# Compression products with the token blocks stationary in four column groups, their weights in a tile of their own, and one product that adds the four parts

## The chip, the cores and the metric

The kernel runs on one NeuronCore of a Trainium2 chip. The metric is the device time of one execution in microseconds (us), taken as the median over several executions. The engines are TensorE (PE, with its weight loads listed apart as PEld), VectorE (DVE), ScalarE (ACT), GpSimd (POOL) and SyncE (SP), which issues most of the transfers.

## The reference

The kernel computes one decoder layer for 256 tokens of width 2048: a mixer of 8 NSA heads and 8 MoBA heads, then cross-attention, then a PEER retrieval over 16384 experts, each followed by a LayerNorm. The change touches one part of the first sub-layer, the compression of the NSA keys and values:

```python
def _compress(raw, pe, w1, w2):
    B, S, G, dk = raw.shape
    c = raw.reshape(B, S // NSA_CMP_STRIDE, NSA_CMP_STRIDE, G, dk)
    blocks = jnp.concatenate([c[:, :-1], c[:, 1:]], axis=2) + pe[:, None, :]
    hid = jax.nn.gelu(jnp.einsum('bnlgd,lde->bnge', blocks, w1))
    return jnp.einsum('bnge,ef->bgnf', hid, w2)
```

It runs once for keys and once for values. Here S is 256, the stride 16, a block 32 tokens (l), the head width 128 (d and e), and there are 2 groups g with 15 blocks n each. So `hid` is a sum over 32 positions l of products with a contraction of 128: (15 x 2 blocks, padded to 32) times (128 x 128 weights of that l). Everything is float32.

## The kernel before

All weights of the first sub-layers come as a stream of slots of 1 MB (128 partitions x 2048 float32). SP loads slot s into place s % 4 of a ring, `ring_raw`. ACT rounds it to `ring_hi` (function `high`, L995), DVE subtracts to get the rest, `ring_lo` (function `low`, L1326), and PE multiplies both parts with the split activations. SP may load slot s when DVE has done slot s - 4 (`lo_ready`, wait at L429 to L432), and ACT may write `ring_hi` of slot s when PE has finished slot s - 4 (`slots_done`).

A column slot (`block_slot`) is one block of 128 output columns: 16 pairs of products, L569 (128x512) and L571 (128x256). ACT copies half of its result out of PSUM (`block_cross`, L1013 and L1015), DVE adds the other half (`block_sum`, L1332), and its semaphore `tb_out` lets PE begin the slot two further on, which uses the same bank. A row slot (`row_slot`, L586) has 24 products of 128x512. The order of the stream at the place of the change is:

- slots 0 to 7: column slots for kc, vc, ks and kw. The first four give `cmpT`, from which DVE builds `blocks` (`blocks_sum`, L1364), 32 tokens positions x 32 columns
- slots 8, 9: the compression weights of the keys (`S_W1K`)
- slots 10 to 17: eight column slots of the NSA queries (`S_NQ`)
- slots 18, 19: the compression weights of the values (`S_W1V`)
- slot 20: the column slot of the gates (`S_GATE`)
- slots 21 to 32: row slots of the values (`S_V`), then the MoBA slots and the rest

The four slots of compression weights are `PLAIN`: ACT and DVE touch only one of their 2048 columns, so that the counts go on, and PE reads them from `ring_raw` as they are. Because PE itself still reads them, SP must wait until PE has done such a slot before it loads the slot four further on:

```python
                if s - R in PLAIN:
                    sp.wait_ge(slots_done, s - R + 1)
```

The 32 products of a compression (L611) have the weights as the stationary operand (128 columns) and `blocks[:, l, :]` (32 columns) as the streaming one, and accumulate in bank 6 or 7. They are interleaved with a column slot: two of them ahead of each of the 16 pairs of slot 10 (keys) and of slot 20 (values). ACT then applies gelu (`hidden`, L1037), and PE multiplies with w2 (L622 for the keys, L650 for the values, over `hid_m`). All orders on the engines are written out by hand; there is no scheduler.

## Time and profile before

| | us |
|---|---|
| median of 3 executions | 1907.45 |
| lowest, highest | 1903.71, 1908.88 |
| span of the profiled execution | 1905.7 |
| PE busy in it | 1866.7 (98%) |
| DVE, ACT, POOL busy | 1459.0, 841.7, 343.3 |

The page of the profile gives no time of its own for the profiled execution beside its span of 1905.7 us; it is 1.75 us below the median. Times in the rows are microseconds from the start of the span. In a row of instructions in order of time, the first number is the start and the second the duration; the ends of matmuls are modelled, and they overlap, so the pace of PE is read from start to start. A product of two plain float32 operands stands in the trace as two weight loads and two matmuls; an operand rounded to fp32r gives one of each.

### The profile page before, as it was taken

The page shows a single profiled execution, that of the slowest core. Times are in us where ns is not written, and L with a number is a line of the kernel's source. Part 1 is how long each engine was busy: PE and PEld are TensorE (multiplying, and loading weights), DVE is VectorE, ACT ScalarE, POOL GpSimd, SP SyncE. Part 2 cuts the span into 40 slices and gives each one's busy share as a digit, 9 for nine tenths or more (in the row PEclk, how much of TensorE's full clock was granted, in tenths as well). Part 3 has the DMA queues.
Part 4 walks back from the last instruction along what each step waited for, and adds up shares of the span by engine and source line. Part 5 has one row for each costly group of instructions (what it writes and reads, how often), then busy time and mean ns, then how long its engine had stood idle before and what let it go on. Part 6 is the DMA issues. An engine that isn't in the chain of part 4 may idle for free.

```text
span 1905.7 us, 25814 instructions
## 1 busy us (share of the span) xinstructions
PE 1866.7 (98%) x10388; PEld 1638.1 (86%) x10388; DVE 1459.0 (77%) x1920; ACT 841.7 (44%) x1138; POOL 343.3 (18%) x216
## 2 busy tenths in 40 slices
PE   7999999999989999999999999999999999999997
PEld 6888888888778999999777889889899898898895
DVE  5444555567674599896888888988988989989886
ACT  4333455444443101223455455455455454454552
POOL 1000122000000001101333223322222323223200
PEclk9999999999989999999999999999999999999999
DMA  8445433755343766889999989999989999989881
GB/s 312 190 168 197 169 118 131 287 193 226 133 155 116 269 251 254 343 338 334 339 361 372 374 342 366 390 352 377 382 349 383 373 350 392 361 359 387 351 318 45
DMA packets 100199, 548.22 MB, mean 288 GB/s; under 512 B 8704, under 2 KB 33344, under 8 KB 35952
## 3 DMA queue, kind: packets, MB, share of 16 engines
q1 hardware_dynamic: 53424, 374.37, 51.5%
q0 software_dynamic: 20096, 147.04, 19.0%
q10 hardware_dynamic: 26560, 25.17, 4.3%
q8 instruction: 82, 1.34, 0.3%
q14 instruction: 37, 0.30, 0.0%
HBM read 530.74 MB, written 14.68 MB: 286 GB/s over the span
## 4 chain that ended last, share of the span: by engine, by line
PE 96%; DVE 1%; ACT 1%; DMA 1%; issue 1%; SPq 0%; POOL 0%; DVEq 0%; ACTq 0%
PE bank L931 14%; PE bank L833 11%; PE bank L569 11%; PE bank L586 9%; PE bank L933 7%; PE bank L864 6%; PE bank L863 6%; PE bank L867 6%; PE bank L865 6%; PE bank L866 6%; PE bank L571 5%; PE bank L853 2%; PE bank L799 1%; DMA ring_raw<-in_stream 1%; PE bank L611 1%
## 5 line engine op out<-in xcount | busy, mean ns | idle before, releaser
L569 PE MATMUL bank<-act_split,ring_hi 128*128 128x512 f32 x896 | 326.1, 406 | 13.9 <-DVE ring_lo L1337 8.0
L1326 DVE TENSOR_TENSOR ring_lo<-ring_raw,ring_hi 128x2048 fp32r<-128x2048 f32 (+1 forms) x94 | 206.5, 2200 | 142.8 <-ACT ring_hi L995 142.6
L1798 DVE TENSOR_TENSOR split_a<-experts,split_a 128x2048 fp32r<-128x2048 f32 x120 | 274.8, 2290 | 52.7 <-ACT split_a L1251 52.3
L1251 ACT CAST split_a<-experts 128x2048 fp32r<-128x2048 f32 x120 | 229.7, 1914 | 139.1 <-PE bank L867 138.4
L931 PE MATMUL bank<-h_split,split_a 128*128 128x384 f32 x944 | 270.8, 359 | 0.0
L571 PE MATMUL bank<-act_split,ring_lo 128*128 128x256 f32 x896 | 252.6, 282 | 0.0
L933 PE MATMUL bank<-h_split,split_a 128*128 128x192 f32 x944 | 236.3, 250 | 0.0
L538 POOL DMA_INDIRECT rows<-in_peer_u,eidx x64 | 139.7, 2183 | 448.3 <-DVE rows L1705 442.6
L538 POOL DMA_INDIRECT rows<-in_peer_v,eidx x64 | 151.1, 2361 | 370.3 <-DVE hrow L1711 346.6
L995 ACT CAST ring_hi<-ring_raw 128x2048 fp32r<-128x2048 f32 (+1 forms) x94 | 172.6, 1837 | 102.1 <-PE bank L586 66.0
L569 PEld LDWEIGHTS bank<-act_split,ring_hi 128*128 128x128 f32 x896 | 170.4, 190 | 54.0 <-DVE act_split L1337 8.0
L833 PE MATMUL bank<-h2T,experts 128*128 128x192 f32 x1280 | 216.3, 326 | 0.0
L833 PEld LDWEIGHTS bank<-h2T,experts 128*128 128x128 f32 x1280 | 206.9, 190 | 0.0
L933 PEld LDWEIGHTS bank<-h_split,split_a 128*128 128x128 f32 x944 | 180.3, 191 | 0.3
L931 PEld LDWEIGHTS bank<-h_split,split_a 128*128 128x128 f32 x944 | 177.1, 188 | 0.7
L571 PEld LDWEIGHTS bank<-act_split,ring_lo 128*128 128x128 f32 x896 | 171.2, 191 | 0.1
L1798 DVE TENSOR_TENSOR split_b<-experts,split_b 128x2048 fp32r<-128x2048 f32 x61 | 139.7, 2289 | 39.9 <-ACT split_b L1251 39.7
L586 PE MATMUL bank<-ring_hi,act_split 128*128 128x512 f32 x512 | 161.3, 394 | 0.0
L1251 ACT CAST split_b<-experts 128x2048 fp32r<-128x2048 f32 x61 | 116.7, 1913 | 82.3 <-PE bank L867 78.0
L1705 DVE SCALAR_TENSOR_TENSOR rows<-rows,hrow 128x2048 f32<-128x2048 f32 x64 | 146.1, 2286 | 3.6 <-DMA rows<-in_peer_u,eidx 3.5
L1711 DVE SCALAR_TENSOR_TENSOR hrow<-rows,wpair,hrow 128x2048 f32<-128x2048 f32 x63 | 147.8, 2347 | 0.0
L931 PE MATMUL bank<-h_split,split_b 128*128 128x384 f32 x464 | 134.1, 359 | 0.0
(273 smaller groups left out, 3449.3 us busy)
## 6 DMA issues: line engine op xcount, KB each, us to landing
experts<-in_stream SPq DMA_DIRECT2D x221, 1024.0 KB, 6.7
ring_raw<-in_stream SPq DMA_DIRECT2D x95, 1024.0 KB, 4.8
late_raw<-in_stream SPq DMA_DIRECT2D x35, 1024.0 KB
gate_matrix<-stage ACTq DMA_DIRECT2D x12, 1024.0 KB
gbuf<-gate_matrix ACTq DMA_DIRECT2D x16, 768.0 KB, 13.2
gb<-in_ln_g POOLq DMA_DIRECT2D x3, 1024.0 KB, 5.1
gb<-in_ln_b POOLq DMA_DIRECT2D x3, 1024.0 KB, 9.3
act_raw<-in_xT SPq DMA_DIRECT2D x4, 512.0 KB, 8.0
```

Of the source, the lines that this page charges most:

```text
L538: pool.indirect_dma_start(rows[:, n % BUFS, :], None, table, bass.IndirectOffsetOnAxis(ap=eidx[:, k:k + 1], axis=0)).then_inc(row_landed[n ...
L569: pe.matmul(bank[n % 2][:, :], hi[:, k * P:(k + 1) * P], act_split[:, k].rearrange("p c t -> p (c t)"), start=(k == 0), stop=False, skip_g ...
L571: last = pe.matmul(bank[n % 2][:, 0:T], lo[:, k * P:(k + 1) * P], actT_hi[:, k, :], start=False, stop=(k == KO - 1), skip_group_check=True)
L586: last = pe.matmul(outs[t][:, :], act[x][:, k, t * P:(t + 1) * P], ring[w][:, r, j * 512:(j + 1) * 512], start=(q == 0 and j == 0 and n == 0),
L833: last = pe.matmul(bank[(N_U + k) % 2][:, 0:ND], experts[:, k % RP, ko * P:(ko + 1) * P], h2T[:, ko, :], start=(ko == 0), stop=(ko == KO - 1))
L931: pe.matmul(b[:, 0:2 * ND], hi[:, w], h2_split[:, ko].rearrange("p c t -> p (c t)"), start=(ko == 0), stop=False, skip_group_check=True)
L933: last = pe.matmul(b[:, 0:ND], lo[:, w], h2_split[:, ko, 0, :], start=False, stop=(ko == KO - 1), skip_group_check=True)
L995: act.copy(ring_hi[:, r, 0:n], ring_raw[:, r, 0:n]).then_inc(hi_ready, 1)
L1251: act.copy(split(m)[0], tile).then_inc(split_hi, 1)
L1326: dve.tensor_tensor(ring_lo[:, r, 0:n], ring_raw[:, r, 0:n], ring_hi[:, r, 0:n].bitcast(F32), ALU.subtract).then_inc(lo_ready, 1)
L1711: ins = dve.scalar_tensor_tensor(out=hrow[:], in0=rows[:, b, :], scalar=wpair[:, k:k + 1], in1=hrow[:], op0=ALU.mult, op1=ALU.add)
L1798: dve.tensor_tensor(lo, raw_slot(split_slot(m))[0], hi.bitcast(F32), ALU.subtract).then_inc(split_lo, 1)
```

## The change

The compression weights leave the stream: it is four slots shorter, and all later slot numbers fall. They get a tile of their own, `w1` (two halves of 128x2048), used first for the keys and then for the values. SP loads its halves behind slots 5 and 6, and again behind slots 14 and 15, the second time after the keys' products. No slot is `PLAIN` any more, and the waits of SP on `slots_done` go.

The operands of the 32 products change places: `blocks[:, l, :]` (32 columns) is stationary, and the 128 columns of the weights stream. Position l writes to the 32 partitions number l % 4 of the bank, so there are four sums of 8 products each, in four column groups of the array. ACT copies the four parts to `quarters` (128x128), and one product with `join` (four 32x32 identities above one another, built once by DVE) adds them and turns them to the layout of before. Each compression is one run of 32 products ahead of a column slot, and its adding product stands behind that slot.

```diff
-PLAIN = (S_W1K, S_W1K + 1, S_W1V, S_W1V + 1)
+W1K_AT, W1V_AT = 5, 14
...
+                sb("below_w1", [P, 12, T], c=c2)
+                w1 = sb("w1", [P, 2, 2048], c=c2)
...
                 sp.wait_ge(lo_ready, s - R + 1)
-                if s - R in PLAIN:
-                    sp.wait_ge(slots_done, s - R + 1)
                 sp.dma_start(ring_raw[:, s % R, :], a["stream"][s]).then_inc(landed[s % R], 16)
+                if s in (W1K_AT, W1K_AT + 1):
+                    sp.dma_start(w1[:, s - W1K_AT, :], a["w1"][s - W1K_AT]).then_inc(w1_landed[s - W1K_AT], 16)
+                if s in (W1V_AT, W1V_AT + 1):
+                    sp.wait_ge(quarter_psum, 1)
+                    sp.dma_start(w1[:, s - W1V_AT, :], a["w1"][2 + s - W1V_AT]).then_inc(w1_landed[s - W1V_AT], 16)
...
-                    if compressed is not None:
-                        compress(compressed, 2 * k)
-                        compress(compressed, 2 * k + 1)
...
-            def compress(kv, l):
-
-                half, j = l // 16, l % 16
-                s = (S_W1K, S_W1V)[kv] + half
-                if l == 0:
-                    pe.wait_ge(blocks_ready, kv + 1)
-                if j == 0:
-                    pe.wait_ge(landed[s % R], 16 * (s // R + 1))
-                last = pe.matmul(bank[6 + kv][:, 0:32], ring_raw[:, s % R, j * P:(j + 1) * P], blocks[:, l, :],
-                                 start=(l == 0), stop=(l == CMP_LEN - 1))
-                if j == 15:
-                    last.then_inc(slots_done, 1)
-
+            def compress(kv):
+
+                pe.wait_ge(blocks_ready, kv + 1)
+                for half in range(2):
+                    pe.wait_ge(w1_landed[half], 16 * (kv + 1))
+                for l in range(CMP_LEN):
+                    half, j, quarter = l // 16, l % 16, l % 4
+                    last = pe.matmul(bank[6 + kv][32 * quarter:32 * quarter + 32, 0:P], blocks[:, l, :],
+                                     w1[:, half, j * P:(j + 1) * P], start=(l < 4), stop=(l >= CMP_LEN - 4))
+                last.then_inc(quarter_psum, 1)
+
+            def join_quarters(kv):
+
+                pe.wait_ge(quarter_ready, kv + 1)
+                if kv == 0:
+                    pe.wait_ge(join_ready, 1)
+                pe.matmul(bank[6 + kv][:, 256:288], quarters[:, kv, :], join[:], start=True, stop=True).then_inc(hid_psum, 1)
+
+            compress(0)
             for b in range(NSA_H):
                 pe.wait_ge(tb_out, N_NQ + b - 1)
-                block_slot(S_NQ + b, N_NQ + b, compressed=0 if b == 0 else None)
+                block_slot(S_NQ + b, N_NQ + b)
+                if b == 0:
+                    join_quarters(0)
...
             pe.wait_ge(const_landed, 32)
             pe.wait_ge(hid_ready, 1)
             pe.matmul(bank[6][:, 128:160], w2[:, 0, :], hidT[:, 0, :], start=True, stop=True).then_inc(kc_psum, 1)
             pe.wait_ge(tb_out, N_GATE - 1)
-            block_slot(S_GATE, N_GATE, compressed=1)
+            compress(1)
+            block_slot(S_GATE, N_GATE)
+            join_quarters(1)
...
-                n = 1 if s in PLAIN else 2048
-                act.copy(ring_hi[:, r, 0:n], ring_raw[:, r, 0:n]).then_inc(hi_ready, 1)
+                act.copy(ring_hi[:, r, :], ring_raw[:, r, :]).then_inc(hi_ready, 1)
...
-                act.wait_ge(slots_done, (S_W1K, S_W1V)[kv] + 2)
-                act.activation(hidT[:, kv, :], bank[6 + kv][:, 0:32], ACT.Gelu_apprx_tanh).then_inc(hid_ready, 1)
-
-            for s in range(S_W1K, S_NQ):
-                high(s + AHEAD)
-            hidden(0)
+                act.wait_ge(hid_psum, kv + 1)
+                act.activation(hidT[:, kv, :], bank[6 + kv][:, 256:288], ACT.Gelu_apprx_tanh).then_inc(hid_ready, 1)
+
+            def quarters_out(kv):
+
+                act.wait_ge(quarter_psum, kv + 1)
+                act.copy(quarters[:, kv, :], bank[6 + kv][:, 0:P]).then_inc(quarter_ready, 1)
+
+            quarters_out(0)
             for b in range(NSA_H):
                 high(S_NQ + b + AHEAD)
                 block_cross(S_NQ + b, N_NQ + b, SCALE)
+                if b == 0:
+                    hidden(0)
             act.wait_ge(kc_psum, 1)
             act.copy(kcT[:], bank[6][:, 128:160]).then_inc(kc_ready, 1)
-            for s in range(S_W1V, S_GATE):
-                high(s + AHEAD)
-            hidden(1)
+            quarters_out(1)
             high(S_GATE + AHEAD)
             block_cross(S_GATE, N_GATE)
+            hidden(1)
...
+            dve.wait_ge(consts, 1)
+            dve.tensor_reduce(join[:], ident[:].rearrange("p (j n) -> p n j", j=4), AX_X, ALU.add).then_inc(join_ready, 1)
...
-            dve.wait_ge(slots_done, S_W1K + 2)
-            blocks_sum(1)
             for s in range(S_NQ, S_GATE):
                 low(s + AHEAD)
-                if s < S_W1V:
-                    block_sum(N_NQ + s - S_NQ, qkT[:, B_NQ + s - S_NQ, :], SCALE)
-
-            dve.wait_ge(hid_ready, 2)
-            st.done(dve.memset(hid_m[:], 0.0))
-            st.settle()
-            for h in range(NSA_H):
-                g = h // (NSA_H // GROUPS)
-                ins = dve.tensor_copy(hid_m[:, h, 16 * h:16 * h + N_CMP], hidT[:, 1, 16 * g:16 * g + N_CMP])
-            ins.then_inc(hidm_ready, 1)
+                block_sum(N_NQ + s - S_NQ, qkT[:, B_NQ + s - S_NQ, :], SCALE)
+                if s == S_NQ + 1:
+                    dve.wait_ge(quarter_psum, 1)
+                    blocks_sum(1)
+
             for s in range(S_GATE, S_V + 5):
                 low(s + AHEAD)
                 if s == S_GATE:
                     block_sum(N_GATE, gateT[:])
+                    dve.wait_ge(hid_ready, 2)
```

How the instructions stand at the places of the change, in the order of the program (L numbers are those of each kernel; x and a number are a count). On PE before, at the end of slot 7 and the start of the queries' first column slot:

```order
L571 MATMUL bank<-act_split,ring_lo 128x256
L611 MATMUL bank<-blocks,ring_raw 128x32 x2
L569 MATMUL bank<-act_split,ring_hi 128x512
L571 MATMUL bank<-act_split,ring_lo 128x256
L611 MATMUL bank<-blocks,ring_raw 128x32 x2
```

On PE now, at the same place (`w` is the tile `w1`):

```order
L577 MATMUL bank<-act_split,ring_lo 128x256
L616 MATMUL bank<-w,blocks 32x128 x32
L575 MATMUL bank<-act_split,ring_hi 128x512
L577 MATMUL bank<-act_split,ring_lo 128x256
L575 MATMUL bank<-act_split,ring_hi 128x512
```

And on PE now, at the end of that slot:

```order
L575 MATMUL bank<-act_split,ring_hi 128x512
L577 MATMUL bank<-act_split,ring_lo 128x256
L625 MATMUL bank<-join,quarters 128x32
L575 MATMUL bank<-act_split,ring_hi 128x512
L577 MATMUL bank<-act_split,ring_lo 128x256
```

The 32 products stood two by two among the pairs of the slot; now they are one run ahead of it, and the adding product stands behind it. The same holds at the slot of the gates.

On SP before, the loads of slots 4 to 96 with what each waits for (one row here is several loads):

```order
L432 DMA ring_raw<-in_stream 128x2048 [waits lo_ready] x8
L432 DMA ring_raw<-in_stream 128x2048 [waits slots_done,lo_ready] x2
L432 DMA ring_raw<-in_stream 128x2048 [waits lo_ready] x8
L432 DMA ring_raw<-in_stream 128x2048 [waits slots_done,lo_ready] x2
L432 DMA ring_raw<-in_stream 128x2048 [waits lo_ready] x73
```

And now (`w<-in_w` is a half of `w1`):

```order
L438 DMA ring_raw<-in_stream 128x2048 [waits lo_ready] x2
L440 DMA w<-in_w 128x2048
L438 DMA ring_raw<-in_stream 128x2048 [waits lo_ready]
L440 DMA w<-in_w 128x2048
L438 DMA ring_raw<-in_stream 128x2048 [waits lo_ready] x8
L443 DMA w<-in_w 128x2048 [waits quarter_psum]
L438 DMA ring_raw<-in_stream 128x2048 [waits lo_ready]
L443 DMA w<-in_w 128x2048 [waits quarter_psum]
L438 DMA ring_raw<-in_stream 128x2048 [waits lo_ready] x77
```

The four loads that waited for PE's slots wait for DVE alone now; two loads of `w1` stand unguarded among the first ones, and two wait for the end of the keys' run. On ACT, the copy of the four parts stands ahead of the cast of slot 11, and the gelu of the keys stands behind the first copy of a query block, where before it stood ahead of it.

## Rows read from the trace of the kernel before

**Rows 1.** Page: chain that ended last, share of the span by engine

```profile
PE 96%; DVE 1%; ACT 1%; DMA 1%; issue 1%; SPq 0%; POOL 0%; DVEq 0%; ACTq 0%
```

**Rows 2.** Waits, 20 to 135 us: who waited for whom; total, times, longest

```profile
PE bank L569 <- DVE qkT L1332: 3.5, 1, 3.5
```

**Rows 3.** SP's own waits, 0 to 160 us

```profile
SPq L431 <- PE bank L611: 56.5, 4, 23.9
```

**Rows 4.** Timeline of ACT, 58 to 90 us: start, us, engine line op

```profile
71.33 1.28 ACT L1037 ACT_TABLE_LOAD   x1
...
75.55 1.90 ACT L995 CAST ring_hi<-ring_raw 128x2048 fp32r<-128x2048 f32 x1 [2.72 <-DMA ring_raw<-in_stream]
```

**Rows 5.** Timeline of PE, 69 to 88 us

```profile
76.12 0.39 PE L569 MATMUL bank<-act_split,ring_hi 128*128 128x512 f32 x1
...
80.16 0.50 PE L569 MATMUL bank<-act_split,ring_hi 128*128 128x512 f32 x1 [3.54 <-DVE qkT L1332]
...
81.68 0.59 PE L569 MATMUL bank<-act_split,ring_hi 128*128 128x512 f32 x1
...
85.32 0.40 PE L569 MATMUL bank<-act_split,ring_hi 128*128 128x512 f32 x1
```

**Rows 6.** Stretches: length; PE, PEld, DVE, ACT, POOL busy; PEclk, DMA share, GB/s

```profile
30.00:35.00 5.00, 5.00 (x31) 4.35 (x30) 2.62 (x2) 2.21 (x2) 0.00 (x0) 1.00 0.99 344
35.00:40.00 5.00, 5.00 (x30) 4.35 (x29) 3.79 (x4) 2.19 (x2) 0.00 (x0) 1.00 0.57 205
80.00:86.00 6.00, 5.84 (x24) 5.04 (x25) 4.84 (x4) 2.12 (x2) 0.00 (x0) 0.72 1.01 421
153.00:161.00 8.00, 8.00 (x28) 6.71 (x28) 3.97 (x6) 1.97 (x3) 0.00 (x0) 0.57 0.46 173
```

**Rows 7.** Timeline of PE, 54 to 62 us

```profile
58.23 0.53 PE L611 MATMUL bank<-blocks,ring_raw 128*128 128x32 f32 x4
```

**Rows 8.** Timeline of PE, 128 to 129.5 us

```profile
128.63 0.40 PE L586 MATMUL bank<-ring_hi,act_split 128*128 128x512 f32 x1
```

**Rows 9.** Timeline of ACT, 20 to 60 us

```profile
27.01 1.92 ACT L995 CAST ring_hi<-ring_raw 128x2048 fp32r<-128x2048 f32 x1 [0.29 <-DMA ring_raw<-in_stream]
...
47.12 0.37 ACT L1013 COPY bcross<-bank 128x256 f32<-128x256 f32 x1 [5.18 <-PE bank L571]
...
58.43 0.37 ACT L1013 COPY bcross<-bank 128x256 f32<-128x256 f32 x1 [3.48 <-PE bank L571]
```

**Rows 10.** Timeline of PE, 115 to 117.2 us

```profile
115.71 0.30 PE L622 MATMUL bank<-hidT,w 128*128 128x32 f32 x2
115.85 0.61 PE L611 MATMUL bank<-blocks,ring_raw 128*128 128x32 f32 x4
```

**Rows 11.** Line L611: duration ns min/median/max, first and last start

```profile
L611 PEld LDWEIGHTS bank<-blocks,ring_raw x128: 187/192/192, 58.1 to 128.1; 128*128 128x128 f32 x128
L611 PE MATMUL bank<-blocks,ring_raw x128: 190/276/276, 58.2 to 128.1; 128*128 128x32 f32 x128
```

**Rows 12.** Timeline of PE, 201 to 204 us

```profile
200.95 1.95 PE L650 MATMUL bank<-w,hid_m 128*128 128x128 f32 x16
202.74 0.38 PE L656 MATMUL bank<-ident,pc 128*128 128x128 f32 x2
```

**Rows 13.** Weight loads by form, whole span: busy us, mean ns

```profile
L863 PEld LDWEIGHTS bank<-split_a,w_split 128*128 128x128 f32 x332 | 62.2, 187 | 30.3 <-issue 0.2
...
L867 PEld LDWEIGHTS bank<-split_a,w_split 128*64 128x64 f32 x332 | 44.5, 134 | 13.9
```

**Rows 14.** Timeline of DVE, 20 to 60 us

```profile
23.72 0.42 DVE L1332 SCALAR_TENSOR_TENSOR cmpT<-bank,bcross 128x256 f32<-128x256 f32 x1 [0.35 <-ACT bcross L1013]
```

**Rows 15.** DVE by form, whole span: busy us, mean ns

```profile
L1326 DVE TENSOR_TENSOR ring_lo<-ring_raw,ring_hi 128x2048 fp32r<-128x2048 f32 x90 | 205.9, 2291 | 142.8 <-ACT ring_hi L995 142.6
...
L1767 DVE TENSOR_REDUCE gsum<-pick 128x8 f32<-128x128 f32 x2 | 0.5, 280 | 0.0
```

**Rows 16.** Timeline of PE, 149 to 161 us

```profile
150.62 4.33 PE L638 MATMUL bank<-kcT,qkT 128*128 128x16 f32 x32
```

More of the change, by code:

```diff
@@ L42 @@
 S_KC = 0
-S_W1K = 8
-S_NQ = 10
-S_W1V = 18
-S_GATE = 20
-S_V = 21
-S_MQK = 33
-S_WOUT = 49
-S_XK = 65
-S_XV = 69
-S_XQ = 73
-S_XO = 77
-S_PQ = 81
+S_NQ = 8
+S_GATE = 16
+S_V = 17
+S_MQK = 29
+S_WOUT = 45
+S_XK = 61
+S_XV = 65
+S_XQ = 69
+S_XO = 73
+S_PQ = 77
 EARLY_G = 5
-S_U0 = 97
+S_U0 = 93
 S_V0 = S_U0 + 8 * EARLY_G
@@ L174, in build @@
             w2 = sb("w2", [P, 2, P], F32, c0)
+            quarters = sb("quarters", [P, 2, P], F32, c0)
+            join = sb("join", [P, 32], F32, c0)
         with ExitStack() as c0:
@@ L315, in build @@
         slots_done = sem("slots_done")
+        w1_landed = [sem(f"w1_landed{i}") for i in range(2)]
+        quarter_psum = sem("quarter_psum")
+        quarter_ready = sem("quarter_ready")
+        join_ready = sem("join_ready")
+        hid_psum = sem("hid_psum")
         tb_out = sem("tb_out")
@@ L1395, in _ @@
                     block_sum(N_GATE, gateT[:])
+                    dve.wait_ge(hid_ready, 2)
+                    st.done(dve.memset(hid_m[:], 0.0))
+                    st.settle()
+                    for h in range(NSA_H):
+                        g = h // (NSA_H // GROUPS)
+                        ins = dve.tensor_copy(hid_m[:, h, 16 * h:16 * h + N_CMP], hidT[:, 1, 16 * g:16 * g + N_CMP])
+                    ins.then_inc(hidm_ready, 1)
             dve.wait_ge(gate_exp, 1)
@@ L1949, in lay_out @@
     stream = np.zeros((N_SLOTS, P, 2048), np.float32)
-    stream[S_KC:S_W1K] = columns(np.concatenate([c[n] for n in ("kc", "vc", "ks", "kw")], axis=1))
-    stream[S_NQ:S_W1V] = columns(c["nq"])
+    stream[S_KC:S_NQ] = columns(np.concatenate([c[n] for n in ("kc", "vc", "ks", "kw")], axis=1))
+    stream[S_NQ:S_GATE] = columns(c["nq"])
     stream[S_GATE].reshape(P, KO, P)[:, :, 0:24] = c["gl"].reshape(KO, P, 24).transpose(1, 0, 2)
@@ L1977, in lay_out @@
         "stream": stream,
+        "w1": w1,
         "xT": turned(f["x"]),
```

14 lines of the change are left out of this document (6 added, 8 removed).

## The prediction, on record before the changed kernel ran

> **What bounds the kernel now.** I read the page first: 96% of the chain that ended last is PE [rows 1]. So time comes off where PE has fewer cycles to spend or stops waiting, and whatever the other engines save is worth nothing by itself. The compression stands between 58 and 129 us. The waits of that stretch show one stop of PE in it: 3.5 us, for DVE's sum of a query block [rows 2]. SP's own waits tell why: four loads waited 56.5 us in all for the products L611, because PE reads the compression weights out of the ring itself [rows 3]. The slots behind them come late, ACT's cast stands idle for a landing at 75.55 [rows 4], and behind that cast stand the copy and the sum for which PE waits; it starts again at 80.16 [rows 5]. Shortly after that stop the granted clock falls to half: it is 0.72 in the mean over 80 to 86 us [rows 6].
>
> **What goes, step by step.** The stretch runs from the first L611 at 58.23 [rows 7] to the first row-slot product at 128.63 [rows 8]: 70.4 us. In it lie nine plain column slots. One takes (58.43 - 47.12) / 2 = 5.655 us, from the copies at their ends [rows 9], or 0.353 us a pair; nine make 50.9. The product with w2 takes 115.85 - 115.71 = 0.14 [rows 10]. The rest is 19.4 us, in three parts:
> - The stop: the last pair starts at 76.12 and would be over at 76.47; the next one starts at 80.16, 3.7 us later, with 0.1 for its slower start [rows 5]. 3.8 us.
> - The low clock behind it: six pairs from 81.68 to 85.32 take 3.64 us in place of 2.12 [rows 5]. 1.5 us.
> - The products themselves: 19.4 - 3.8 - 1.5 = 14.1 us, 7.05 a compression. The values' one by itself is 128.63 - 115.85 - 5.655 = 7.13 [rows 8, 10]. 128 matmuls for 64 products [rows 11] are two per product, so 64 per compression at 110 ns each. A matmul with 32 streaming columns is short; the load of 128 weight columns sets this pace.
>
> **What comes in its place.** Now 128 columns stream and 32 are loaded. The nearest row is L650, plain float32 with 128 columns on either side: 16 matmuls from 200.95 to 202.74, 112 ns each [rows 12]. No row shows two column groups at work at once, so I bound it:
> - Lower end: all four groups stream side by side. 64 / 4 x 0.112 = 1.8 us a compression.
> - Upper end without a further loss: nothing is side by side. 64 x 0.112 = 7.2 us, as much as before.
> - Beyond it: the load isn't hidden either. Loads of 128 and of 64 columns last 187 and 134 ns [rows 13], 53 ns for 64 columns, so 107 ns for a load of 32 from start to end, and 64 x 0.219 = 14.0 us.
>
> I take half: 3.6 us. Each product is two matmuls on the same column group, one behind the other, and PE takes matmuls in the program's order. The second can't stream before the first has, but the next product's first, on another group, can stream beside it. Two groups are then busy on average, and a product costs 0.112 us: 32 x 0.112 = 3.6.
>
> The Trainium skill speaks for some overlap and against it. Its page "TensorEngine Tiling (Array Packing)", section "Key Properties", says that tiles can load and multiply in parallel, and that a change of the tiling mode drains the engine. Its page "TensorE: Matmul & The Clock Gate", section "The mechanism", says that a weight load overlaps running matmuls only where the row groups differ; here all four groups use all rows. Taken word for word that is the 14.0 us case, a rival below. The rows of before do not bear it out for full-width loads: at 110 ns a matmul with loads of 187 ns and more [rows 11], loads do run ahead on the same rows.
>
> At either edge of a run the array changes its form. No row prices that: it is between nothing and a whole matmul's duration, 0.28 us for L611 [rows 11], so up to 1.1 us at four edges; I take 0.1 each. The adding product has the shape of the one with w2, which took 0.14 [rows 10]; with an edge of its own I allow 0.3. That is 1.0 us for both compressions. New cost: 2 x 3.6 + 1.0 = 8.2. Gain: 19.4 - 8.2 = 11.2 us.
>
> **Edits that I cost at nothing, and their cover.** Times are of the changed kernel, PE's run from 58.2 to 61.8.
> - The copy to `quarters` stands on ACT ahead of the cast of slot 11. At some 0.37 us, the copy of twice as many columns [rows 9], it ends at 62.2; cast (1.9 us, [rows 9]) and subtraction (2.3 us, [rows 15]) end near 66.5. PE begins slot 11 at 61.8 + 3 x 5.655 = 78.8. Cover 12 us.
> - The adding product waits for that copy; PE reaches it at 61.8 + 5.7 = 67.5. Cover 5 us. Behind it on PE stands the whole next slot, so without the cover each us late costs one.
> - The gelu stands with its table load (1.3 us, [rows 4]) on ACT ahead of the cast of slot 12, which is then ready at 74, and PE needs it at 84. For the values, gelu and the building of `hid_m` stand ahead of DVE's subtraction of slot 20, some 3 us later than it could be, and PE needs slot 20 three row slots later, 16 us.
> - SP moves the first two halves of `w1` ahead of slots 6 and 7. At 344 GB/s a MB takes 3.0 us, and the transfers are nearly full until 35 us and not behind it [rows 6]. Slot 5 is still ahead of them; ACT's cast of it already waited 0.3 us for its landing at 27.01 [rows 9]. Slot 6 lands up to 3 us later, is ready by about 38 to 39, and PE begins it at 47.12 (the copy of slot 5's block, [rows 9]). Slot 7 has the same 8 us. `w1` itself is there by 38, twenty us before its use.
> - The values' halves wait for the end of the keys' run, behind which SP has slot 15 to load; that one waits for DVE until about 66 anyway.
> - DVE's reduction for `join` takes about 0.28 us [rows 15] in a gap of 0.35 us in which DVE waits for ACT [rows 14]. If it runs over, PE's stop before slot 2 grows by 0.1.
> - The waits of SP on PE are gone; next in line is `lo_ready`, which holds no load long enough for PE to see it: slot 11 to 13 come ten us early.
>
> Everything behind 129 us moves forward as it stands, since 96% of the chain is PE [rows 1] and loads there are released by work that moves with it.
>
> The sum for the profiled execution: span 1905.7 - 11.2 = 1894.5. The page shows no time around the span; the median of the runs is 1.75 us above it, so 1907.45 - 11.2 = **1896.2 us**.
>
> **The rivals.**
> - *Four wide.* The second matmul of a product does not hold the queue. 1.8 us a compression: gain 19.4 - 3.6 - 1.0 = 14.8, time 1892.6. For it: the program puts neighbours on four different groups. Against it: the order inside a product.
> - *No overlap, load hidden.* 7.2 us a compression: only the stop and the low clock are won, 19.4 - 14.4 - 1.0 = 4.0, time 1903.4. For it: no row shows two groups at once, and the pace of before is one matmul after another.
> - *The clock falls behind the run.* The run of 32 small matmuls L638 at 150.62 [rows 16], 4.3 us long, is followed by a granted clock of 0.57 over 153 to 161 us, a loss of 8 x 0.43 = 3.4 us [rows 6]. Before, the compression was mixed with full products and no such fall is seen behind it. As a block by itself it could bring the fall once or twice: 1896.2 + 3.4 = 1899.6, or 1903.0. Where the fall behind L638 stays away instead, the forecast loses 3.4 and is 1892.8.
> - *Slower: the load is not hidden.* PE loads a column group only when it is still. 14.0 us a compression: 19.4 - 28.0 - 1.0 = -9.6, time 1917.1. The point from which it decides is a matmul's pace of (19.4 - 1.0) / 128 = 144 ns, and 188 ns for more than 0.3%. Against it: the pace of L611.
> - *The gain is given back*, the expert stream of the last stage being late by as much: 1907. Against it: the share of DMA in the chain is 1% [rows 1].
>
> **How the numbers follow.** About 0.3%, 5.7 us, is what a measurement of this kernel can tell from no change: below 1901.7 is faster, above 1913.2 slower. Forecast 0.40, four wide 0.17, no overlap 0.23, clock 0.09, load not hidden 0.07, given back 0.04. Faster: all of the forecast's and four wide's 0.57, two thirds of the clock's, and about a fifth of the no-overlap case, whose time is 1.7 above the bound: 0.68. Slower: the unhidden load and a bit of mishap, 0.08. The rest, 0.24, is the same. The forecast's own range is 1892 to 1900. For 8 in 10 I reach from four wide with the fall gone (1889.5) to the end of the no-overlap case (1906.5), which leaves out the slower rival, the given-back case and little else.
>
> **What would show it.** L616 should have 128 loads and 128 matmuls, with starts 56 ns apart in a run of 3.6 us; 28 ns would be four wide, 112 no overlap, 219 an unhidden load. PE's idle for `qkT` near 76 us and the granted clock below 1 there should be gone, SP should wait for PE no more in this stretch, and nine slots should still take 5.65 us each. The forecast is wrong if the run's pace differs, if ACT or DVE wait for landings of slots 6 to 8 long enough for PE to stop, or if the granted clock drops behind a run.

## The result and the profile after

The changed kernel takes 1890.62 us in the median of 4 executions (1889.16 to 1891.21), the kernel before 1908.16 us beside it. The ratio is 0.9917, with a 95% interval of 0.9903 to 0.9931: 15.8 us faster, between 13.2 and 18.5. The forecast was 1896.2 us and a gain of 11.2. The direction and the range (1889.5 to 1906.5) held; the gain is about 40% larger than forecast.

The profiled execution has a span of 1888.8 us, 16.9 below the one before. Its run for the keys and the adding product, in PE's timeline (start, duration, engine, line, operation), answer to [rows 7] and [rows 11]:

```profile
59.41 0.27 PE L577 MATMUL bank<-act_split,ring_lo 128*128 128x256 f32 x1
59.62 1.96 PE L616 MATMUL bank<-w,blocks 128*32 128x128 f32 x64
61.50 0.50 PE L575 MATMUL bank<-act_split,ring_hi 128*128 128x512 f32 x1
...
67.26 0.30 PE L625 MATMUL bank<-join,quarters 128*128 128x32 f32 x2
67.40 0.48 PE L575 MATMUL bank<-act_split,ring_hi 128*128 128x512 f32 x1
```

64 matmuls lie between 59.62 and 61.50, 1.88 us. The last pair of slot 7 starts at 59.18 and, at 0.35 us a pair, would be over at 59.53, so the run costs 1.97 us of PE with both edges, where it cost 7.05 before. The values' run, from 107.29 us on, has the same length. The adding product takes 0.14, like the product with w2 of before.

The waits of PE in 20 to 130 us, answering to [rows 2], and those of SP in 0 to 160 us, answering to [rows 3]:

```profile
PE bank L575 <- DVE cmpT L1350: 2.7, 1, 2.7
```

```profile
SPq L438 <- DVE ring_lo L1344: 124.1, 25, 8.0
...
SPq L443 <- PE bank L616: 2.6, 1, 2.6
```

PE stops only once, at the start of the kernel, as it did before too; the stop for `qkT` is gone. SP waits for DVE, and for PE only where it holds back the values' weights. The busy times by stretch (columns as in [rows 6]) show the granted clock:

```profile
24.00:30.00 6.00, 5.45 (x22) 4.70 (x23) 5.25 (x4) 4.12 (x4) 0.00 (x0) 0.72 1.02 420
80.00:86.00 6.00, 6.00 (x36) 5.21 (x35) 2.72 (x2) 2.53 (x3) 0.00 (x0) 1.00 0.65 229
137.00:147.00 10.00, 10.00 (x63) 8.92 (x62) 3.96 (x6) 4.91 (x6) 0.00 (x0) 1.00 0.58 209
```

It is full over 80 to 86 us, where it was 0.72, and full behind the scores of the compressed branch, where it was 0.57. It was low already inside their run before: that lasted 4.33 us [rows 16] and lasts 3.64 now. But it is 0.72 at 24 to 30 us, where it was full before. The end of the stretch, answering to [rows 8], and the scores, answering to [rows 16]:

```profile
115.07 0.48 PE L592 MATMUL bank<-ring_hi,act_split 128*128 128x512 f32 x1
```

```profile
137.16 3.64 PE L654 MATMUL bank<-kcT,qkT 128*128 128x16 f32 x32
140.65 0.48 PE L592 MATMUL bank<-ring_hi,act_split 128*128 128x512 f32 x1
```

Cut at these places, the 16.9 us between the two profiled executions divide as follows. L650 of before (L666 now) marks the end of the fourth part; it starts at 200.95 before [rows 12] and at 184.29 now.

| part of the span | before | after | gained |
|---|---|---|---|
| start to the first compression matmul | 58.23 | 59.62 | -1.4 |
| from there to the first row-slot product | 70.40 | 55.45 | 14.95 |
| from there to the scores | 21.99 | 22.09 | -0.1 |
| scores to L650 | 50.33 | 47.13 | 3.2 |
| the rest | 1704.8 | 1704.5 | 0.2 |

So 14.95 us belong to the stretch of the change. The 3.2 and most of the -1.4 are low clocks that fell otherwise in the two executions; what they have to do with the change is a question for the experiments.

### The profile page after: what moved, and what is told of

The parts are those of the page before. It is cut to its first block, busy times and chain, and to the rows that moved or that the text cites. A ratio compares the mean times of both kernels' runs of the same rounds, so it can differ in the third digit from the quotient of the medians.

```text
span 1888.8 us, 25810 instructions
## 1 busy us (share of the span) xinstructions
PE 1852.9 (98%) x10392; PEld 1625.5 (86%) x10392; DVE 1459.4 (77%) x1917; ACT 841.4 (45%) x1136; POOL 345.4 (18%) x216
## 3 DMA queue, kind: packets, MB, share of 16 engines
q8 instruction: 82, 1.34, 0.3%
## 4 chain that ended last, share of the span: by engine, by line
PE 96%; DVE 1%; ACT 1%; DMA 1%; issue 1%; SPq 0%; POOL 0%; DVEq 0%; ACTq 0%
PE bank L947 15%; PE bank L849 11%; PE bank L575 11%; PE bank L592 9%; PE bank L949 7%; PE bank L880 6%; PE bank L883 6%; PE bank L881 6%; PE bank L879 6%; PE bank L882 6%; PE bank L577 5%; PE bank L869 2%; PE bank L815 1%; DMA ring_raw<-in_stream 1%; PE bank L682 0%
## 5 line engine op out<-in xcount | busy, mean ns | idle before, releaser
L575 PE MATMUL bank<-act_split,ring_hi 128*128 128x512 f32 x896 | 319.4, 400 | 10.9 <-DVE ring_lo L1355 8.2
L1344 DVE TENSOR_TENSOR ring_lo<-ring_raw,ring_hi 128x2048 fp32r<-128x2048 f32 x90 | 205.9, 2290 | 137.3 <-ACT ring_hi L1010 136.9
L1010 ACT CAST ring_hi<-ring_raw 128x2048 fp32r<-128x2048 f32 x90 | 171.8, 1909 | 80.9 <-PE bank L592 72.0
```

What stands on the lines that cost most here:

```text
L575: pe.matmul(bank[n % 2][:, :], hi[:, k * P:(k + 1) * P], act_split[:, k].rearrange("p c t -> p (c t)"), start=(k == 0), stop=False, skip_g ...
L1010: act.copy(ring_hi[:, r, :], ring_raw[:, r, :]).then_inc(hi_ready, 1)
L1344: dve.tensor_tensor(ring_lo[:, r, :], ring_raw[:, r, :], ring_hi[:, r, :].bitcast(F32), ALU.subtract).then_inc(lo_ready, 1)
```

## The experiments

Ratios are against the kernel before, on the same chip and beside each run; PE's pieces are from the profiles. "Own home" is the tile `w1` for the weights.

| kernel | ratio (95%) | median us | length of the keys' run, us |
|---|---|---|---|
| changed kernel, second time | 0.9921 (0.9907 to 0.9934) | 1890.7 | 1.88 |
| own home, products of before, interleaved | 0.9970 (0.996 to 0.998) | 1899.6 | |
| own home, products of before in one run | 1.0015 (1.0004 to 1.0026) | 1909.1 | 10.6 |
| four groups, weights in the ring | 0.9937 (0.9924 to 0.995) | 1893.8 | 1.89 |
| the same, other order on ACT and DVE | 0.9916 (0.9903 to 0.993) | 1889.7 | 1.88 |
| two groups alternating | 0.9928 (0.9914 to 0.9943) | 1892.3 | 3.22 |
| eight products in a row on a group | 0.9966 (0.9953 to 0.9979) | 1899.0 | 5.88 |
| two products in a row on a group | single run | 1890.4 | 1.95 |
| four products in a row on a group | single run | 1896.8 | 4.26 |
| changed kernel, scores spread | 0.9911 (0.9898 to 0.9925) | 1889.1 | 1.88 |
| the same, and an earlier first sum | 0.9917 (0.9903 to 0.993) | 1889.6 | 1.89 |
| kernel before, second profile | single run | 1907.2 | |

**The home alone.** The products of before, interleaved as before, with the weights in `w1`:

```diff
-                last = pe.matmul(bank[6 + kv][32 * quarter:32 * quarter + 32, 0:P], blocks[:, l, :],
-                                 w1[:, half, j * P:(j + 1) * P], start=(l < 4), stop=(l >= CMP_LEN - 4))
+                last = pe.matmul(bank[6 + kv][:, 0:32], w1[:, half, j * P:(j + 1) * P], blocks[:, l, :],
+                                 start=(l == 0), stop=(l == CMP_LEN - 1))
...
```

> The weights have their home of their own, but the products are those of before: weights stationary (128 columns), 32 columns streaming, two by two among the pairs of a column slot; no parts, no adding product. Theory (the gain has two separate sources, and this one is the ring's): PE's stop near 76 us and the low clock behind it go, 3.8 + 1.5 = 5.3 us, the products still cost 7.05 us each; 1908.2 - 5.3 = 1902.9, and about 1899.5 where the clock does not fall behind L638. Rival (the stop is gone in the changed kernel only because its runs are short, so that the home alone is worth nothing): 1908, with a stop of PE for the sum of a query block near 76 us.

Measured: 0.9970, 5.7 us below before (3.8 to 7.6); the theory's 5.3 lies well inside. The run is not the home alone, though: ACT and DVE keep the order of the changed kernel, with the gelu of the keys behind the first copy of a query block and the blocks of the values built later. So it prices the home together with that order. PE's only wait in 20 to 130 us is the one at the start:

```profile
PE bank L578 <- DVE cmpT L1340: 2.7, 1, 2.7
```

**Groups alone, weights in the ring.** The run of four groups reads slots 8, 9 and 18, 19 of the ring, and these are `PLAIN` again:

```diff
...
-                                     w1[:, half, j * P:(j + 1) * P], start=(l < 4), stop=(l >= CMP_LEN - 4))
-                last.then_inc(quarter_psum, 1)
...
+                                         ring_raw[:, (s + half) % R, j * P:(j + 1) * P], start=(l < 4), stop=(l >= CMP_LEN - 4))
+                    last.then_inc(slots_done, 1)
...
```

> The four column groups and the adding product as in the changed kernel, one run ahead of the slot, but the weights still come in the ring (slots 8, 9 and 18, 19), and SP waits for PE before it loads four slots further on. Theory A (a run of 1.9 us gives the ring slots back by about 60 us, not 64 and 71, so their successors come in time): no stop of PE, the same as the changed kernel, 1890.6 within 1.5. Theory B (the home of its own is what removes the stop): a stop of about 3.5 us with a low clock behind it, 1890.6 + 5.3 = 1895.9.

Measured: 0.9937, some 3 us slower than the changed kernel at 0.9921, each against the kernel before on its own chip, and between the two theories; the two intervals overlap, so the 3 us are not clear of noise. A stop is left, but a short one:

```profile
73.01 0.50 PE L571 MATMUL bank<-act_split,ring_hi 128*128 128x512 f32 x1 [1.44 <-DVE qkT L1352]
```

In the timelines of ACT and DVE the sum for which PE waits stands behind other work. That stop is 1.4 us, and no low clock follows it; the rest of the 3 us was not traced, and the profiled execution was the shortest of the five. ACT's third cast waits for a landing at 67.84, its copy comes at 69.66, and DVE builds the second blocks and subtracts before it sums at 72.53:

```profile
67.84 1.91 ACT L1008 CAST ring_hi<-ring_raw 128x2048 fp32r<-128x2048 f32 x1 [1.95 <-DMA ring_raw<-in_stream]
69.66 0.37 ACT L1028 ACTIVATE bcross<-bank 128x256 f32<-128x256 f32 x1
```

```profile
68.13 2.05 DVE L1386 TENSOR_TENSOR blocks<-cmpT,pe_raw 128x512 f32<-128x512 f32 x2
70.33 2.29 DVE L1346 TENSOR_TENSOR ring_lo<-ring_raw,ring_hi 128x2048 fp32r<-128x2048 f32 x1
72.53 0.42 DVE L1352 SCALAR_TENSOR_TENSOR qkT<-bank,bcross 128x256 f32<-128x256 f32 x1
```

**The same with another order on ACT and DVE.** The first query block is copied and summed ahead of the next cast and subtraction, and the blocks of the values are built later:

```diff
             for b in range(NSA_H):
-                high(S_NQ + b + AHEAD)
+                if b:
+                    high(S_NQ + b + AHEAD)
                 block_cross(S_NQ + b, N_NQ + b, SCALE)
                 if b == 0:
                     hidden(0)
+                    high(S_NQ + b + AHEAD)
...
-            dve.wait_ge(slots_done, S_W1K + 2)
-            blocks_sum(1)
             for s in range(S_NQ, S_GATE):
-                low(s + AHEAD)
+                if s > S_NQ:
+                    low(s + AHEAD)
                 if s < S_W1V:
                     block_sum(N_NQ + s - S_NQ, qkT[:, B_NQ + s - S_NQ, :], SCALE)
+                if s == S_NQ:
+                    low(s + AHEAD)
+                if s == S_NQ + 1:
+                    dve.wait_ge(slots_done, S_W1K + 2)
+                    blocks_sum(1)
```

> Four groups with the weights in the ring, as in the run with the ring, and besides the order of the changed kernel: ACT copies the first query block ahead of its next cast, DVE sums it ahead of its next subtraction, and builds the second set of blocks two blocks later. Theory (the stop of 1.4 us left in the run with the ring came from casts, subtractions and the building of the blocks that stand ahead of the sum, not from the ring): no stop near 71 us, the same as the changed kernel within 1.5 us, so that the home of its own is worth nothing once the run is short. Rival (late loads of the ring are enough for a stop): a stop of 1 us or more stays, and the time stays 2 us or more above the changed kernel.

Measured: 0.9916, the same as the changed kernel beside it (0.9921). The sum comes at 68.41, and PE has no stop there:

```profile
68.41 0.42 DVE L1354 SCALAR_TENSOR_TENSOR qkT<-bank,bcross 128x256 f32<-128x256 f32 x1
```

```profile
PE bank L571 <- DVE cmpT L1354: 2.1, 1, 2.1
```

SP still waits for PE there, 35.8 us in all, and PE does not feel it:

```profile
SPq L436 <- PE bank L613: 35.8, 4, 18.9
```

So the stop of before had two ways out, and the home is only one. With a run of 1.9 us the ring gives its slots back soon enough; what stopped PE then was the order on the two helpers.

A third way was not run: the kernel before with this order alone. Its rows, of ACT and then of DVE, speak for it:

```profile
72.63 0.20 ACT L1037 ACTIVATE hidT<-bank 128x32 f32<-128x32 f32 x1
...
77.35 0.38 ACT L1015 ACTIVATE bcross<-bank 128x256 f32<-128x256 f32 x1
```

```profile
71.35 2.29 DVE L1326 TENSOR_TENSOR ring_lo<-ring_raw,ring_hi 128x2048 fp32r<-128x2048 f32 x1 [8.42 <-ACT ring_hi L995]
...
79.69 0.42 DVE L1332 SCALAR_TENSOR_TENSOR qkT<-bank,bcross 128x256 f32<-128x256 f32 x1
```

The copy at 77.35 waits behind the late cast, not for PE, whose products of that block were over by 71 us. Put directly behind the gelu and the subtraction, copy and sum would be done near 74 (an estimate from these rows), and PE stops only at 76.5. So neither the home nor the short run is shown to be needed against the stop.

**Eight products in a row on a group.** The same instructions in another order of groups:

```diff
-                    half, j, quarter = l // 16, l % 16, l % 4
+                    half, j, quarter = l // 16, l % 16, l // 8
                     last = pe.matmul(bank[6 + kv][32 * quarter:32 * quarter + 32, 0:P], blocks[:, l, :],
-                                     w1[:, half, j * P:(j + 1) * P], start=(l < 4), stop=(l >= CMP_LEN - 4))
+                                     w1[:, half, j * P:(j + 1) * P], start=(l % 8 == 0), stop=(l % 8 == 7))
```

> The changed kernel with its 32 products in another order of column groups: eight in a row on the first group, then eight on the second, and so on. Same instructions, same sums. Theory (PE takes matmuls in order, and what runs side by side is only what neighbours on different groups give): one group streams at a time, 64 x 0.112 = 7.2 us a run, 1890.6 + 2 x (7.2 - 1.9) = 1901.2. Rival (PE looks further ahead than its neighbours, or a short load alone made the run fast): 1.9 us a run, 1890.6.

**Two groups alternating:**

```diff
-                    half, j, quarter = l // 16, l % 16, l % 4
+                    half, j, quarter = l // 16, l % 16, l % 2 + 2 * (l // 16)
                     last = pe.matmul(bank[6 + kv][32 * quarter:32 * quarter + 32, 0:P], blocks[:, l, :],
-                                     w1[:, half, j * P:(j + 1) * P], start=(l < 4), stop=(l >= CMP_LEN - 4))
+                                     w1[:, half, j * P:(j + 1) * P], start=(l % 16 < 2), stop=(l % 16 >= 14))
```

> The changed kernel with its products alternating between two column groups only (0 and 1 in the first half of the run, 2 and 3 in the second). Theory (time goes as the number of groups that stream at once, and the two matmuls of a product do not hold back the next group): 64 / 2 x 0.107 = 3.5 us a run, 1890.6 + 2 x (3.5 - 1.9) = 1893.8. Rival (the two matmuls of a product do hold the queue as the prediction said, and the trace's four at once come from something else): with two groups some 5 us or more a run, 1897 and up.

Measured: 5.88 and 3.22 us a run, and ratios that follow, 0.9966 and 0.9928. The rival of the first had two halves. One, that a short load alone does it, falls; the other, that PE looks further ahead than its neighbours, holds in part. For 5.88 is less than the 7.0 of one group at a time. The matmuls of a run counted by stretches of 1 us (columns: length, busy PE, count, busy PEld, count, granted clock, DMA share, GB/s), first for the eight in a row, then for the two groups, then for the changed kernel:

```profile
59.44:60.44 1.00, 1.00 (x9) 1.00 (x10) 1.00 0.89 164
60.44:61.44 1.00, 1.00 (x15) 1.00 (x14) 1.00 0.95 401
```

```profile
59.45:60.45 1.00, 0.99 (x18) 1.00 (x20) 1.00 0.50 123
60.45:61.45 1.00, 1.00 (x30) 1.00 (x28) 1.00 1.02 434
```

```profile
59.60:60.60 1.00, 0.98 (x36) 0.98 (x40) 1.00 0.72 156
60.60:61.60 1.00, 0.97 (x36) 0.70 (x28) 1.00 0.91 377
```

In the first microsecond they are as 9 to 18 to 36: one, two and four groups, each with a matmul every 109 ns. In the second one the eight in a row have 15. The starts in the trace show where the surplus lies: single matmuls every 109 ns up to the 12th, then pairs from 1.34 us on, four of them, then single ones again. The trace does not name the group of a matmul, but each group gets 16. So this is read as the next group's first starting with the 13th, while three wait at the old group. Three changes of group save 3 x 4 x 0.109 = 1.3 us of 7.0, which is what is measured (5.7, and 0.2 at the edges). With two groups alternating there is one such change: 3.5 - 0.44 = 3.05, and 0.2 at the edges makes 3.2.

**Two and four products in a row on a group,** to test that reading with a number given ahead:

```diff
-                    half, j, quarter = l // 16, l % 16, l % 4
+                    half, j, quarter = l // 16, l % 16, l // 2 % 4
                     last = pe.matmul(bank[6 + kv][32 * quarter:32 * quarter + 32, 0:P], blocks[:, l, :],
-                                     w1[:, half, j * P:(j + 1) * P], start=(l < 4), stop=(l >= CMP_LEN - 4))
+                                     w1[:, half, j * P:(j + 1) * P], start=(l < 8 and l % 2 == 0), stop=(l >= CMP_LEN - 8 and l % 2 == 1))
```

> The changed kernel with two products (four matmuls) in a row on each column group before the next group's. Theory (each group takes its own matmuls one after another at 109 ns, and PE goes on to the next group while up to three wait at a group; read from the order with eight products in a row, where the second group's first matmul starts together with the 13th of 16): four still fit, so all groups run and a run takes 16 x 0.109 + 0.1 = 1.9 us, as in the changed kernel. Rival (PE looks ahead by four matmuls over all groups together): two groups at a time at best, 3.5 us.

> The same with four products (eight matmuls) in a row on each group. Theory of the waiting places: a group's block of eight lets the next group begin when its fifth starts, every 4 x 0.109 = 0.44 us; eight blocks give 7 x 0.44 + 8 x 0.109 = 3.9 us, and 4.0 with the edges, two groups at a time. Rival (no such places, PE takes matmuls in order and only neighbours overlap): 64 x 0.109 = 7.0 less 7 neighbours, 6.2 us. Rival (a window far deeper): 1.9 us.

Measured: 1.95 and 4.26 us:

```profile
59.43 2.02 PE L616 MATMUL bank<-w,blocks 128*32 128x128 f32 x64
61.38 0.50 PE L575 MATMUL bank<-act_split,ring_hi 128*128 128x512 f32 x1
```

```profile
59.79 4.33 PE L616 MATMUL bank<-w,blocks 128*32 128x128 f32 x64
64.05 0.50 PE L575 MATMUL bank<-act_split,ring_hi 128*128 128x512 f32 x1
```

The rivals with other numbers (3.5; 6.2 or 1.9) fall. A step from group to group took 0.466 us and not 0.436, which makes 4.1 without the edges. Each length is from one profile, and the values' run has the same. The reading stands: PE goes on to another group while up to three matmuls wait at one.

**The products of before in one run.** Own home, form of before, place of the changed kernel:

```diff
-                    if compressed is not None:
-                        compress(compressed, 2 * k)
-                        compress(compressed, 2 * k + 1)
+                if compressed is not None:
+                    for l in range(CMP_LEN):
+                        compress(compressed, l)
...
```

> Own home, the products of before (128 weight columns stationary, 32 columns streaming), but all 32 in one run ahead of the slot, as the changed kernel has them. It parts the place of the products from their form. Theory: 64 loads of 128 columns at 110 ns, 7.05 us a run, so the time of the same kernel with the products interleaved, 0.997 of before or 1900. Rival (a run of small matmuls by itself brings the low clock, which the interleaving before prevented): the granted clock falls behind one or both runs, up to 3.4 us each, 1903 to 1907.

Measured: 1.0015, 8.6 us above the interleaved form (1.0015 - 0.9970 = 0.0045 of 1905.8 us), and slower than the kernel before, though it has no stop in the stretch. The rival was right, and its price too low. The two runs take 10.6 us (57.27 to 67.86) and 9.4, not 7.05:

```profile
57.27 10.78 PE L619 MATMUL bank<-blocks,w 128*128 128x32 f32 x64
67.86 0.77 PE L578 MATMUL bank<-act_split,ring_hi 128*128 128x512 f32 x1
```

```profile
57.00:60.00 3.00, 3.00 (x29) 2.96 (x27) 0.75 (x2) 2.17 (x2) 0.00 (x0) 1.00 0.82 287
60.00:70.00 10.00, 10.00 (x48) 9.71 (x48) 1.97 (x1) 0.00 (x0) 0.00 (x0) 0.52 0.14 40
...
118.00:128.00 10.00, 10.00 (x43) 9.33 (x43) 0.41 (x1) 0.00 (x0) 0.00 (x0) 0.52 0.28 106
```

PE is busy without a gap in all of it, and the granted clock is 0.52 over 60 to 70 and over 118 to 128 us, the lower level of 1.2 GHz nearly throughout. The two runs are 5.9 us longer than 2 x 7.05, and the rest of the loss falls on the column slots behind them, in which the clock stays low at first. Both runs whose matmuls stream 32 columns behind loads of 128 lost the clock; the same products two by two between full ones did not, and a run with 32 loaded columns and 128 streaming ones did not either, not even with one group at a time for 5.9 us.

**The scores spread.** The 16 score products behind the first products of the row slot, one each:

```diff
+                            if between:
+                                between.pop(0)()
                             last = pe.matmul(outs[t][:, :], act[x][:, k, t * P:(t + 1) * P],
...
```

> The changed kernel with the 16 score products of the compressed branch (L654: 128 weight columns, 16 streaming) spread one by one over the first 16 products of the row slot that followed them. Theory (the run of these small matmuls brings the low clock behind it in some executions, at 3.4 us): never a low clock between 135 and 160 us, mean time 0 to 2 us below the changed kernel and less spread. Rival (the fall comes from elsewhere or is too rare): the same time as the changed kernel within 0.5 us.

Measured: 0.9911, not to be told from the changed kernel beside it (0.9921). Its granted clock is full where the scores stand:

```profile
137.00:147.00 10.00, 10.00 (x63) 8.90 (x62) 4.11 (x6) 4.81 (x6) 0.00 (x0) 1.00 0.61 211
147.00:157.00 10.00, 10.00 (x46) 8.29 (x45) 6.37 (x8) 3.69 (x3) 0.00 (x0) 1.00 0.30 105
```

**The changed kernel and the one before, a second time:**

> The changed kernel once more, on the same chip as the runs beside it. 0.9917 of the kernel before, 1890 where before is 1906. Its profile is another look at where the granted clock falls: theory (the falls of one gap of some 3 us near 24 us and behind the scores L654 come and go from execution to execution, since they hang on how the stretches lie in time): one or the other place differs from the first profile. Rival (the change itself took the fall behind the scores away): no fall there again, as in the first profile.

> The kernel before once more, for a second profile. Theory (the fall of the clock behind L638 comes and goes): with or without it; the stop of 3.5 us near 76 us and the products at 110 ns are there in either case, and in the sum the span is 1902 to 1907. Rival (the fall belongs to the kernel before): it is there again, 6.8 us long.

```profile
24.00:30.00 6.00, 5.83 (x33) 5.17 (x34) 4.93 (x4) 4.10 (x3) 0.00 (x0) 1.00 1.01 419
137.00:147.00 10.00, 10.00 (x47) 8.39 (x47) 3.96 (x6) 3.45 (x4) 0.00 (x0) 0.83 0.44 151
```

```profile
24.00:30.00 6.00, 5.84 (x24) 4.97 (x25) 4.93 (x4) 4.09 (x3) 0.00 (x0) 0.72 1.01 369
80.00:86.00 6.00, 4.39 (x16) 3.77 (x17) 5.93 (x5) 3.78 (x3) 0.00 (x0) 0.72 1.00 423
151.00:161.00 10.00, 10.00 (x48) 8.78 (x48) 3.96 (x6) 4.37 (x5) 0.00 (x0) 0.66 0.66 250
```

The changed kernel has its low clock behind the scores this time and not at the start; from the scores to L666 it takes 48.7 us, against 47.1. The kernel before has one at the start now, and those near 80 us and behind the scores again. Over the twelve profiles with the scores in one run the clock fell behind them at a loss of some 3.2 us in five, at 1.6 in two and not at all in five. Near 25 us it fell in eight of all fourteen. Instructions around these places are alike in the kernels, so these falls come and go. The one near 25 us goes with the length of PE's stop for `cmpT` ahead of it: it came in all seven profiles in which that stop was 2.7 us or 2.8, and in one of the seven in which it was between 1.6 and 2.4. That of before near 82 us was there in both its profiles and never elsewhere.

From the first compression matmul to the first row-slot product this pair of profiles takes 69.8 us (59.72 to 129.50) and 55.4 us (57.65 to 113.09). The difference is 14.3, against 14.95 in the first pair. What parts the two pairs is the pace of the full column slots, to be read between ACT's copies at their ends. Ahead of the run and behind it in the changed kernel, in its first profile:

```profile
54.18 0.37 ACT L1028 COPY bcross<-bank 128x256 f32<-128x256 f32 x1 [3.37 <-PE bank L577]
59.73 0.37 ACT L1028 COPY bcross<-bank 128x256 f32<-128x256 f32 x1 [3.37 <-PE bank L577]
...
84.64 0.39 ACT L1030 ACTIVATE bcross<-bank 128x256 f32<-128x256 f32 x1 [3.47 <-PE bank L577]
90.29 0.39 ACT L1030 ACTIVATE bcross<-bank 128x256 f32<-128x256 f32 x1 [3.46 <-PE bank L577]
```

And with the own home and the products of before:

```profile
88.89 0.38 ACT L1022 ACTIVATE bcross<-bank 128x256 f32<-128x256 f32 x1 [3.37 <-PE bank L580]
94.44 0.38 ACT L1022 ACTIVATE bcross<-bank 128x256 f32<-128x256 f32 x1 [3.37 <-PE bank L580]
```

A slot takes 5.55 us at one place and 5.65 at another, at full granted clock in both. In all ten profiles with a run on column groups the slots behind it take 5.65 us; in five of them those ahead took 5.55. With the own home and the products of before they take 5.55 on either side. The kernel before had 5.65 throughout in its first profile, and 5.55 behind the stop in its second. No run isolates what sets the pace.

**An earlier first sum,** on top of the spread scores:

```diff
-                high(n + AHEAD)
-                if n == 0:
-                    act.wait_ge(act_lo, A_X)
+                if n:
+                    high(n + AHEAD)
+                else:
+                    act.wait_ge(act_lo, A_X)
                 block_cross(n, n)
+                if n == 0:
+                    high(n + AHEAD)
...
             for s in range(4):
                 block_sum(s, cmpT[:, s, 0:T])
+                if s == 0:
+                    st.done(dve.memset(cmpT[:, :, T:], 0.0))
+                    dve.wait_ge(consts, 1)
+                    dve.tensor_reduce(join[:], ident[:].rearrange("p (j n) -> p n j", j=4), AX_X, ALU.add).then_inc(join_ready, 1)
```

> The changed kernel with the score products spread over the row slot and, at the start, ACT's copy and DVE's sum of the first column slot ahead of the next cast, the clearing of the margin and the reduction for the adding product. Theory: PE's stop near 22 us shrinks by some 0.5 us, and the low clock behind it and behind the scores comes less often: 0.5 to 2 us below the changed kernel, 1888 to 1890 where that is 1890.7. Rival (the stop is set by the split of slot 2, which comes with its landing): no difference that can be told, 1889 to 1891.

Measured: 0.9917, no difference that can be told from the changed kernel, though PE's stop at the start is shorter (1.6 us against 2.7) and the profiled execution, 1885.1 us, is the shortest of all:

```profile
PE bank L575 <- DVE cmpT L1359: 1.6, 1, 1.6
```

No version beats the changed kernel by more than the measurement tells.

## Why the prediction was right or wrong

- *The stop and the low clock behind it, 5.3 us.* Right in size. The home, with the order of the helpers that came with it, gave 5.7 (3.8 to 7.6), and neither is in the profile after. The reason given, that SP waits for PE, was half of it: with the weights in the ring SP waits 35.8 us for PE and no stop comes, once the sum stands ahead.
- *The old products, 14.1 us.* Right. The kernel with the home alone takes 64.4 us in the stretch (59.36 to 123.80); less nine slots at 5.55 and 0.14 for w2 that leaves 14.4, or 7.2 each.
- *The new run, 3.6 us.* Wrong, and this is the term that was mis-sized: 1.88 us, or 1.97 with its edges, against 3.6 + 0.2. The step that failed is "the second can't stream before the first has", taken together with "PE takes matmuls in the program's order". The first half is true: a group gives a matmul every 109 ns. But a waiting matmul does not hold the queue. Up to three wait at their group while PE goes on to the next, so the two matmuls of a product cost nothing in width, and all four groups stream. The rival "four wide", given 0.17, had it: 14.8 us against 14.95 and 14.3 measured in the stretch.
- *Edges 0.1 each and adding product 0.3.* The last matmul starts at 61.30 and would be over at 61.41; the pair begins at 61.50. Both edges are 0.09. The adding product took 0.14. In all 0.6 where 1.0 was allowed. The first pairs behind the runs and the adding products are slower by 0.2 in all, which no term had.
- *The load of 32 columns.* The trace does not agree with the rule of the Trainium skill, page "TensorE: Matmul & The Clock Gate", section "The mechanism", that a load overlaps running matmuls only in other row groups: all four groups use the same rows, and no load is to be seen in the pace of 109 ns. The same section also lets a load go ahead if it targets a background weight buffer; no run here shows whether that is what happens. Its page "TensorEngine Tiling (Array Packing)", section "Theoretical Speedup", names up to four times for four tiles; 64 x 0.109 = 7.0 against 16 x 0.109 = 1.74 is that.
- *Edits at nothing.* All held. The sum behind `join` began as soon as ACT's copy was over; slots 6 and 7 came in time; PE waits for nothing new.
- *Nine slots at 5.65 us.* Held in the changed kernel behind the run, but 5.55 was possible: the home alone had it. Eight slots at 0.1 are 0.8 us, and the stretch fell by 9.0 from the home alone to the changed kernel (64.4 to 55.4), where 14.1 - 4.4 = 9.7 would be expected. Whether the change itself gives this back, as the ten profiles suggest, stays open.
- *The clock behind the run.* It did not fall in any profile with 128 streaming columns. The suspicion was right for the form of before: in one run it costs 8.6 us.
- *The sum.* 19.4 us to be won and 8.2 to be paid; measured 19.4 - 4.4 = 15.0. The ratio's 15.8 us is 0.8 above that. Luck with the clock elsewhere is a candidate; the interval (13.2 to 18.5) can't show it. The range's lower end should read 1889.2 by the prediction's own terms (1892.6 - 3.4), not 1889.5, which changes nothing.

What stays open: what sets the two paces of a column slot; whether the order of the helpers alone would have removed the stop; and why the clock falls behind the scores in some executions and not in others. Two profiles with the scores spread show no fall, but neither do five of twelve without.

## What to carry to other kernels

Small plain float32 products are cheap where the small operand is the loaded one and neighbours write to different column groups; keep no more than four matmuls in a row on a group. Do not gather products with few streaming columns in a run: mix them with full ones, or swap their operands, since such a run can lose much of its worth to the clock: 8.6 us for two of them here. Before giving a tile a home of its own to free a ring, look whether a shorter use and the order of the helpers do the same. When an experiment is to price one part of a change, check that no other part of it came along.

## What the hardware showed that was not expected

- A matmul on a column group of 32 with 128 streaming float32 columns starts every 109 ns on its group, and matmuls on other groups start 7 ns behind one another.
- About four matmuls fit at a group, one that runs and three that wait, before PE stops taking more: runs of 1.9, 1.95, 4.26 and 5.88 us for one, two, four and eight products in a row on a group.
- With PE busy all the time, a run of 64 matmuls with 32 streaming columns brought the granted clock to 0.52 over ten microseconds, twice in one profile; a run with 128 streaming columns on a quarter of the array did not.
- Full column slots have two paces, 5.55 and 5.65 us, both at full granted clock; behind a run on column groups it was 5.65 in all ten profiles.
